# Input stages: four weight sums of a 7-product block scheme become additions, and the fourth is made by two accumulating DMAs

## The reference, cut to what matters

```
h = rms_norm(x, g)                       # 256 x 2048
gate, up = jnp.split(h @ w_in, 2, -1)    # w_in: 2048 x 11264
return (silu(gate) * up) @ w_out
```

## Time and profile before

| | |
|---|---|
| median of 2 runs | 1805.05 us |
| the runs | 1804.71 and 1805.38 us |
| span of the profiled execution | 1802.5 us |
| PE busy | 1797.3 us |
| DVE busy | 1550.1 us |
| ACT busy | 1071.0 us |
| POOL busy | 43.6 us |
| read from HBM | 348.91 MB, 195 GB/s over the span |

### The profile page before, as it was taken

The page is one execution under the profiler, slowest core; times in us unless marked ns, Lnnn a source line. Parts: engine busy times, 40 slices in busy tenths (PEclk is TensorE's granted clock), DMA queues, the critical chain, the costliest instruction groups (busy, mean ns, idle before and its releaser), DMA issues.

```text
span 1802.5 us, 22784 instructions
## 1 busy us (share of the span) xinstructions
PE 1797.3 (100%) x8227; PEld 1491.7 (83%) x8227; DVE 1550.1 (86%) x1614; ACT 1071.0 (59%) x1295; POOL 43.6 (2%) x73
## 2 busy tenths in 40 slices
PE   9999999999999999999999999999999999999999
PEld 8888888888888888888888888888888888888887
DVE  7899999999999887657766666799999999998986
ACT  7566656666665564556556555566666666666553
POOL 0000000000000000111010000000000000000000
PEclk9999999999999999999999999999999999999999
DMA  9565555554446566555545445755566656354654
GB/s 358 214 220 199 207 212 186 196 200 163 140 166 253 189 218 212 198 172 164 164 164 187 143 165 183 257 194 203 191 216 215 215 189 219 104 187 163 240 203 141
DMA packets 178406, 351.95 MB, mean 195 GB/s; under 512 B 7184, under 2 KB 8224, under 8 KB 178080
## 3 DMA queue, kind: packets, MB, share of 16 engines
q1 hardware_dynamic: 178304, 351.02, 55.9%
q10 hardware_dynamic: 32, 0.01, 0.0%
HBM read 348.91 MB, written 2.10 MB: 195 GB/s over the span
## 4 chain that ended last, share of the span: by engine, by line
PE 100%; DVE 0%; ACT 0%; POOL 0%; issue 0%; ACTq 0%; POOLq 0%
PE acc L537 14%; PE acc L539 14%; PE acc L538 13%; PE acc L599 8%; PE acc L598 8%; PE acc L597 8%; PE turn L610 4%; PE turn L611 4%; PE turn L612 4%; PE acc L611 3%; PE acc L612 3%; PE acc L610 3%; PE turn L568 1%; PE turn L714 1%; PE turn L713 1%; PE turn L712 1%
## 5 line engine op out<-in xcount | busy, mean ns | idle before, releaser
L1323 DVE TENSOR_TENSOR w_lo<-w_raw,w_hi 128x1024 fp32r<-128x1024 f32 x167 | 205.0, 1237 | 132.9 <-ACT w_hi L942 132.3
L942 ACT ACTIVATE w_hi<-w_raw 128x1024 fp32r<-128x1024 f32 x166 | 175.4, 1059 | 198.9 <-PE acc L539 177.1
L959 ACT ACTIVATE w_hi<-b 128x1024 fp32r<-128x1024 f32 x200 | 212.6, 1063 | 117.5 <-PE acc L599 75.7
L973 ACT ACTIVATE w_hi<-w_raw 128x1024 fp32r<-128x1024 f32 x176 | 185.3, 1058 | 121.3 <-PE acc L539 88.5
L599 PE MATMUL acc<-w_hi,h_lo 128*128 128x512 f32 x640 | 249.0, 389 | 0.0
L597 PE MATMUL acc<-w_hi,h_hi 128*128 128x512 f32 x640 | 249.0, 389 | 0.0
L598 PE MATMUL acc<-w_lo,h_hi 128*128 128x512 f32 x640 | 249.0, 389 | 0.0
L1344 DVE TENSOR_TENSOR w_lo<-w_raw,w_hi 128x1024 fp32r<-128x1024 f32 x176 | 212.8, 1221 | 32.1 <-ACT w_hi L973 28.5
L1334 DVE TENSOR_TENSOR w_lo<-b,w_hi 128x1024 fp32r<-128x1024 f32 x200 | 236.3, 1218 | 0.0
L959 ACT ACTIVATE w_hi<-w_raw 128x1024 fp32r<-128x1024 f32 x160 | 169.6, 1061 | 91.7 <-PE acc L599 64.1
L1334 DVE TENSOR_TENSOR w_lo<-w_raw,w_hi 128x1024 fp32r<-128x1024 f32 x160 | 193.5, 1220 | 14.7 <-ACT w_hi L959 11.7
(11 more groups left out here) (218 smaller groups left out, 3276.4 us busy)
## 6 DMA issues: line engine op xcount, KB each, us to landing
w_raw<-in_ffn_w_in SPq DMA_DIRECT2D x94, 1024.0 KB, 5.1
w_raw<-in_ffn_w_out SPq DMA_DIRECT2D x88, 1024.0 KB, 5.0
b<-in_ffn_w_in SPq DMA_DIRECT2D x80, 1024.0 KB, 5.1
w_raw<-in_w_in SPq DMA_DIRECT2D x48, 1024.0 KB, 5.0
w_raw<-in_w_out SPq DMA_DIRECT2D x16, 1024.0 KB, 5.0
w_raw<-in_ffn_w_in SPq DMA_DIRECT2D x4, 512.0 KB, 6.6
x_sb<-in_x SPq DMA_DIRECT2D x3, 512.0 KB, 8.7
out_y<-x_sb SPq DMA_DIRECT2D x3, 512.0 KB, 8.5
```

Of the source, the lines that this page charges most:

```text
L942: nc.scalar.activation(w_hi[:, u % RING, 0:count, :], w_raw[:, slot, k0:k0 + count, :], ACT.Copy).then_inc(hi_ready, 1)
L959: nc.scalar.activation(w_hi[:, slot, :, :], in_raw(piece)[:, k0:k0 + UK, :], ACT.Copy).then_inc(hi_ready, 1)
L973: nc.scalar.activation(w_hi[:, u % RING, :, :], src, ACT.Copy).then_inc(hi_ready, 1)
L1323: nc.vector.tensor_tensor(w_lo[:, slot, 0:count, :], w_raw[:, v // 2 % RAW, k0:k0 + count, :], w_hi[:, slot, 0:count, :].bitcast(F32), ALU ...
```

## The change

In the input stages all sums of weights become additions: `t_1 = b_12 + b_11`, `b_12 = b_22 + b_12`, `t_1 = b_22 + t_1`. The signs move to the activation sums (`signed_sums` in place of `activation_sums` for these stages) and to two of the adds of partial products, which become subtractions. The fourth sum, `b_21 + t_1`, is no longer made by DVE. POOL waits until unit 13's `w_lo` is made (the last reader of sum 3) and then issues two DMAs with `accum_op=ADD`, 2 of the 4 rows each, 512 KB, that read B21 from HBM a second time and add it onto `t_1`. ACT waits for each half (`full_sum_landed`) before it converts unit 18 or 19. B21's own load stays, for P2. P4 and P7 change places: P7 is units 16 and 17, P4 units 18 and 19. B12 is now free at 18 and B21 at 11, but the order of the loads becomes ..., B22, B12, B21, U1. DVE splits units 14 to 16 before it adds P6, 17 to 20 before it adds P7, and waits for unit 19's use before it adds the gate bank.

```
-P1, P5, UP0, P2, UP1, P6, P3, P4, P7, UP2 = 4, 6, 8, 9, 11, 12, 14, 16, 18, 20
+P1, P5, UP0, P2, UP1, P6, P3, P7, P4, UP2 = 4, 6, 8, 9, 11, 12, 14, 16, 18, 20
-FREED = {G0: 2, G1: 4, B11: 6, U0: 12, B22: 16, B21: 18, B12: 20, U1: 22}
+FREED = {G0: 2, G1: 4, B11: 6, U0: 12, B22: 16, B12: 18, B21: 11, U1: 22}
...
+                    elif w in (P4, P4 + 1):
+                        act.wait_ge(full_sum_landed[w - P4], at(16, 16 * (IN_LOOPS * n + 1 + later)))
...
-                weight_sum(t_1[:, :, :], b_22[:, :, :], t_1[:, :, :], ALU.subtract)
-                split_in_lo(s_in, i, half, 9, 14)
-                dve.wait_ge(sum_ready, at(4, sums + 3))
-                dve.wait_ge(lo_ready, at(IN_UNITS, u0 + P2 + 2))
-                weight_sum(b_21[:, :, :], b_21[:, :, :], t_1[:, :, :], ALU.subtract)
-                split_in_lo(s_in, i, half, 14, 18)
+                weight_sum(t_1[:, :, :], b_22[:, :, :], t_1[:, :, :], ALU.add)
+                split_in_lo(s_in, i, half, 9, 17)
                 dve.wait_ge(units_used, at(IN_UNITS, u0 + P6 + 2))
                 dve.wait_ge(partial_copied, at(3, copies + 1))
                 add(rows[:, 1, 0, :], partial[0], rows[:, 0, 0, :]).then_inc(partial_copied, 1)
-                split_in_lo(s_in, i, half, 18, 22)
+                split_in_lo(s_in, i, half, 17, 21)
...
-                split_in_lo(s_in, i, half, 22, 23)
+                split_in_lo(s_in, i, half, 21, 23)
+                dve.wait_ge(units_used, at(IN_UNITS, u0 + P4 + 2))
...
+            def full_sums(src, s_in, n):
+                for i in range(IN_LOOPS):
+                    col = (i + 1) * NC
+                    pool.wait_ge(lo_ready, UNIT[s_in] + IN_FIRST + IN_UNITS * i + P6 + 2)
+                    for h in range(2):
+                        k = K_PLAIN + KS + UK * h
+                        nc.gpsimd.dma_start(t_1[:, UK * h:UK * (h + 1), :], src[:, k:k + UK, col:col + NC],
+                                            accum_op=ALU.add).then_inc(full_sum_landed[h], 16)
```

More of the change, by code:

```diff
@@ L62 @@
 IN_RAW = ((G0, 0), (G0, 2), (G1, 0), (G1, 2), (B11, 0), (B11, 2), (T1, 0), (T1, 2), (U0, 0), (B21, 0), (B21, 2),
-          (U0, 2), (T1, 0), (T1, 2), (B22, 0), (B22, 2), (B21, 0), (B21, 2), (B12, 0), (B12, 2), (U1, 0), (U1, 2))
+          (U0, 2), (T1, 0), (T1, 2), (B22, 0), (B22, 2), (B12, 0), (B12, 2), (T1, 0), (T1, 2), (U1, 0), (U1, 2))
 IN_UNITS = len(IN_RAW)
-P1, P5, UP0, P2, UP1, P6, P3, P4, P7, UP2 = 4, 6, 8, 9, 11, 12, 14, 16, 18, 20
-SUM_OF = {P5: 1, P5 + 1: 1, P6: 3, P6 + 1: 3, P4: 4, P4 + 1: 4, P7: 2, P7 + 1: 2}
-FREED = {G0: 2, G1: 4, B11: 6, U0: 12, B22: 16, B21: 18, B12: 20, U1: 22}
+P1, P5, UP0, P2, UP1, P6, P3, P7, P4, UP2 = 4, 6, 8, 9, 11, 12, 14, 16, 18, 20
+SUM_OF = {P5: 1, P5 + 1: 1, P6: 3, P6 + 1: 3, P7: 2, P7 + 1: 2}
+IN_SUMS = 3
+FREED = {G0: 2, G1: 4, B11: 6, U0: 12, B22: 16, B12: 18, B21: 11, U1: 22}
 assert 2 * IN_UNITS % RING == 0 and K_PLAIN == 2 * KT and IN_LOOPS == 2 * IN_PAIRS and KS == KT
@@ L92 @@
 OUT_LANDED = [2 + len(PERIODS)] * 2 + [2 + len(PERIODS) + N_LONG] * 2
-SUMS = 4 * IN_LOOPS + 4 * len(PERIODS)
+SUMS = IN_SUMS * IN_LOOPS + 4 * len(PERIODS)
 ROUNDS = FFN_ITERS
@@ L308, in hybrid_layer_kernel @@
         sum_ready = sem("sum_ready")
+        full_sum_landed = [sem(f"full_sum_landed{h}") for h in range(2)]
         partial_copied = sem("partial_copied")
@@ L456, in ffn @@
                     load(down, a, k, KT, 2, at + X2 + 1)
-                    sp.wait_ge(sum_ready, SUMS * n + 4 * (IN_LOOPS + m + 1))
+                    sp.wait_ge(sum_ready, SUMS * n + IN_SUMS * IN_LOOPS + 4 * (m + 1))
                     load(down, a, j, KT, 0)
@@ L699, in hidden @@
                 form(s_in, u0, half, P3, sum_of(4), banks[1][:, 0, :], False, False)
-                form(s_in, u0, half, P4, block_of(1, 1), banks[0][:, 1, :], False, True)
                 pe.wait_ge(partial_copied, at(3, 3 * IN_LOOPS * n + 2))
                 form(s_in, u0, half, P7, sum_of(3), partial[0], True, True)
+                form(s_in, u0, half, P4, block_of(1, 1), banks[0][:, 1, :], False, True)
                 for v in range(UP2, IN_UNITS):
@@ L951, in split_in_hi @@
                     if w in SUM_OF:
-                        act.wait_ge(sum_ready, at(4, SUMS * n + SUM_OF[w]))
+                        act.wait_ge(sum_ready, at(IN_SUMS, SUMS * n + SUM_OF[w] + IN_SUMS * later))
+                    elif w in (P4, P4 + 1):
+                        act.wait_ge(full_sum_landed[w - P4], at(16, 16 * (IN_LOOPS * n + 1 + later)))
                     elif piece < B11:
@@ L967, in split_out_hi @@
                     if made:
-                        act.wait_ge(sum_ready, SUMS * n + 4 * IN_LOOPS + made)
+                        act.wait_ge(sum_ready, SUMS * n + IN_SUMS * IN_LOOPS + made)
                     else:
@@ L1034, in copy_m1 @@
                 else:
-                    act.wait_ge(sum_ready, SUMS * n + 4 * (IN_LOOPS + m + 1))
+                    act.wait_ge(sum_ready, SUMS * n + IN_SUMS * IN_LOOPS + 4 * (m + 1))
                 act.wait_ge(units_used, UNIT[s_out] + period_at(m) + Q1 + 1)
@@ L1426, in hidden @@
                 dve.wait_ge(block_landed[B12 - B11], landed)
-                weight_sum(t_1[:, :, :], b_12[:, :, :], b_11[:, :, :], ALU.subtract)
+                weight_sum(t_1[:, :, :], b_12[:, :, :], b_11[:, :, :], ALU.add)
                 split_in_lo(s_in, i, half, 4, 5)
                 dve.wait_ge(block_landed[B22 - B11], landed)
-                dve.wait_ge(sum_ready, at(4, sums + 1))
-                weight_sum(b_12[:, :, :], b_22[:, :, :], b_12[:, :, :], ALU.subtract)
+                dve.wait_ge(sum_ready, at(IN_SUMS, sums + 1))
+                weight_sum(b_12[:, :, :], b_22[:, :, :], b_12[:, :, :], ALU.add)
                 split_in_lo(s_in, i, half, 5, 9)
                 dve.wait_ge(lo_ready, at(IN_UNITS, u0 + P5 + 2))
-                weight_sum(t_1[:, :, :], b_22[:, :, :], t_1[:, :, :], ALU.subtract)
-                split_in_lo(s_in, i, half, 9, 14)
-                dve.wait_ge(sum_ready, at(4, sums + 3))
-                dve.wait_ge(lo_ready, at(IN_UNITS, u0 + P2 + 2))
-                weight_sum(b_21[:, :, :], b_21[:, :, :], t_1[:, :, :], ALU.subtract)
-                split_in_lo(s_in, i, half, 14, 18)
+                weight_sum(t_1[:, :, :], b_22[:, :, :], t_1[:, :, :], ALU.add)
+                split_in_lo(s_in, i, half, 9, 17)
                 dve.wait_ge(units_used, at(IN_UNITS, u0 + P6 + 2))
@@ L1446, in hidden @@
                 add(rows[:, 0, 1, :], partial[0], rows[:, 1, 0, :]).then_inc(partial_copied, 1)
-                add(rows[:, 1, 0, :], partial[1], rows[:, 1, 0, :])
+                nc.vector.tensor_tensor(rows[:, 1, 0, :], partial[1], rows[:, 1, 0, :], ALU.subtract)
                 dve.wait_ge(partial_copied, at(3, copies + 3))
-                add(rows[:, 1, 1, :], partial[1], rows[:, 0, 1, :]).then_inc(partial_added, 1)
+                nc.vector.tensor_tensor(rows[:, 1, 1, :], partial[1], rows[:, 0, 1, :],
+                                        ALU.subtract).then_inc(partial_added, 1)
                 if ending:
                     round_act(n, 0)
-                split_in_lo(s_in, i, half, 22, 23)
+                split_in_lo(s_in, i, half, 21, 23)
+                dve.wait_ge(units_used, at(IN_UNITS, u0 + P4 + 2))
                 dve.wait_ge(partial_added, at(1, done))
@@ L1472, in activation_wide, with signed_sums @@
                 return [wide[:, KS * half:KS * (half + 1), t * P:(t + 1) * P] for half in range(2) for t in range(TT)]
+            def signed_sums(raw, a_11, a_21, a_12, a_22):
+                link(nc.vector.tensor_tensor(raw[:, 0], a_21, a_22, ALU.subtract))
+                nc.vector.tensor_tensor(raw[:, 2], a_11, a_21, ALU.subtract)
+                link(nc.vector.tensor_tensor(raw[:, 1], raw[:, 0], a_11, ALU.subtract))
+                nc.vector.tensor_tensor(raw[:, 3], a_12, raw[:, 1], ALU.add).then_inc(s_raw_ready, 1)
             def activation_sums(raw, a_11, a_21, a_12, a_22):
@@ L1527, in ffn @@
                     split_lo(s_in, 8, 10, PARTS_D)
-                    activation_sums(s_raw, *blocks)
+                    signed_sums(s_raw, *blocks)
                     split_lo(s_in, 10, 11, PARTS_D)
@@ L1570, in begin_products @@
                 u0, at = period_at(m), UNIT[s_out] + period_at(m)
-                made = SUMS * n + 4 * (IN_LOOPS + m)
+                made = SUMS * n + IN_SUMS * IN_LOOPS + 4 * m
                 b_11, b_12, b_22 = w_raw[:, 0, 0:UK, :], w_raw[:, 1, 0:UK, :], w_raw[:, 1, UK:KT, :]
@@ L1903, in _ @@
             pool.wait_ge(col_ready, 3)
+            full_sums(tiled(ffn1_w_in), IN1, 0)
             pool.wait_ge(units_used, UNIT[QKV])
@@ L1929, in _ @@
                 nc.gpsimd.tensor_tensor(x2, temps[2], temps[3], ALU.add).then_inc(qk_normed, 1)
+            full_sums(tiled(ffn2_w_in), IN2, 1)
 _INS = ["x", "ffn1_norm", "ffn1_w_in", "ffn1_w_out", "mix_norm", "w_in", "a_q_norm", "a_k_norm", "b_q_norm",
```

## The result

The changed kernel takes 1984.52 us (1984.45 to 1984.59, 2 runs) against 1805.05 us: a ratio of 1.0995, 95% interval 1.0976 to 1.1014. It is slower by 179.5 us, 9.0 us for each of the 20 periods. The profiled execution has a span of 1982.7 us, 180.2 us more than before.

A forecast was written before the change was run, and what follows sets the result against it. PE, busy 1797.3 of 1802.5 us, was taken to bound the kernel. Half 1 landing late stalls PE 2.4 us in each of 20 periods, 48 us: span 1850.5, plus 2.6 around it, 1853 us; range 1803 to 1930.

The forecast's parts named there:

- PE bounds the kernel, DVE's relief is worth 0: Input stages: PE never waits for a weight, so removing 20 DVE sums of 2283 ns, 45.7 us, gains 0.
- The new order: P7 before P4: DVE's add of P6 ends 0.7 us before PE asks for it at unit 16; cost 0.
- The cover: Time from POOL's wait ending to when half 0 and half 1 must have landed: 7.3 and 8.7 us.
- POOL's issue, 1.04 us, and half 0's transfer, 4.9 us: POOL issues half 0 at 329.1; counted as 1 MB of reads, it lands at 334.0, in time by 1.4 us.
- Half 0 goes out at 329.1, half 1 at 330.2: POOL issues the two halves one behind the other, 1.04 us for each, range 0.37 to 2 us.
- rival 2: Halves go one at a time, or adder at half rate (1957 us); stall over 4 us, 1885 to 2000 us; chance 0.28.
- the case without it: The forecast's own case: stall of 1 to 4 us a period, 1825 to 1885 us; chance 0.43.
- Contention, 2.6 us: B22's load shares the DMA engines with half 1, moving its landing from 336.6 to 339.2, late by 2.4 us.
- Rival 3, the clock: PE's clock falls in the stalls, perhaps 1 to 3 us a period on top; no chance of its own, within 0.28.

## Why the prediction was wrong

The forecast was 1853 us with a range to 1930; 1984.5 us came. Step by step:

- *PE bounds the kernel, DVE's relief is worth 0*: right. The run with plain copies takes away the same DVE work and ends at 0.9995 of before.
- *The new order costs 0*, with 0.7 us left at unit 16: right. In the changed kernel the add of P6 ends at 289.92 and unit 16's first weight load starts at 290.66; and the run with the fourth sum on DVE takes as long as before.
- *The cover*, 7.3 and 8.7 us: right. Half 0 landed 6.4 us after the split and did not stall PE. With half 1 at 9.1 us the stalls were small; at 16.1 us PE stood for 7.46 us, close to 16.1 - 8.7.
- *POOL's issue, 1.04 us, and half 0's transfer, 4.9 us*: 5.9 us from the split by the sum; measured, half 0 landed 6.0 us after the issue's start and 6.4 us after the split, which POOL followed after 0.35 us. The sum takes a half for 1 MB of reads, which no row of the kernel before shows. In time it came out right: accumulating halves move about 205 GB/s where a load moves about 400, and the size of the packets is not the reason, since the loads' packets (351.02 MB in 178304) are as small as the accumulating ones (20.97 MB in 10880). That it is a second read is the reading that fits a factor of two; no view shows the reads.
- *"Half 0 goes out at 329.1, half 1 at 330.2"*: this step failed. Half 1 went out 6.36 us after half 0, not 1.04, since with a store of 1024 POOL issued an accumulating half only when the one before had landed. A store of 2048 brings the issues to 0.73 us apart and removes 153 us. I had one half at a time in rival 2, but with 0.28 beside slow adders, when the kernel text gave the parameter. With 0.43 for the case without it, I took the unknown at its kind end.
- *Contention, 2.6 us*: its kind was right and the size depends on the moment. Half 1 met three loads in place of one: 9.4 us to land against 5.9 with the loads held. In the case for which I had computed it (both halves at once) it was smaller than I said: landing at 9.1 us after the split, not 11.1, and PE's waits of 18.4 us in all, not 48. There half 1 took 8.1 us from its issue, against 7.7 with the loads held (289.63 to 297.37), so the term was 0.4 us in these periods and not 2.6. The forecast for that case, 1853 us, compares with 1831.
- *Rival 2's price*: with the prediction's own terms half 1 goes out at 334.0 + 1.04 and lands 4.9 us later at 339.9, with contention at 342.5, a stall of 5.8 us: 20 x 5.8 = 116 us, 1921 us. The waits were 131 us. In the period shown half 1 landed 16.1 us after the split where these terms give 14.4: the issue came 0.8 us later than their sum says (6.7 us after the split, not 5.9), and contention was 3.4 us in place of 2.6.
- *Rival 3, the clock, "perhaps 1 to 3 us a period"*: 2.2 us, 44 us in all. I named it and said that it was left in the range, but no row stood behind these 1 to 3 us, and no term of it went into the upper end. Rivals 2 and 3 are not independent: the long wait is what brings the low clock (0.51 behind 7.46 us of standing, 1.000 over the span when PE was kept busy through it). Added, 1921 + 44 = 1965, they come near the result.

What the runs say of the store can be put as an estimate from the packets of POOL's queue: 272 for an accumulating half (10880 in 40), 144 for an accumulating quarter (11520 in 80) or a plain half (5760 in 40). A limit on the packets under way anywhere from 432 to 543 gives all four outcomes at 1024: two accumulating halves (544) do not go out together, three quarters (432) do, four (576) don't, two plain halves (288) do. Twice such a limit takes the two accumulating halves of the run with 2048. That the store's size is the cause is shown (1984.52 to 1831.08 us by this parameter alone); that it works by this count is not. The fourth quarter does not fit it: with quarter 0 landed at 285.2, 288 packets would be under way and 144 more would fit, but it went out at 288.19, behind the landing of quarter 1.

## What to carry to other kernels

Before a second DMA of POOL is counted as running right behind the first, make sure that it is issued before the first has landed; here, with `dynamic_dma_scratch_size=1024`, two plain halves went out back to back (1.45 us for both) and two accumulating ones 6.36 us apart. When an engine has no waits, taking work from its neighbours is worth nothing (with the plain copies DVE had the same relief, at 0.9995 of the time before), and a new transfer in the chain is priced by latency against its window, at the moment when other loads run. A wait of several microseconds on TensorE is priced with the slow matmuls behind it: here 2.2 us on 7.5.

## What the runs showed of the hardware that I had not expected

- With `dynamic_dma_scratch_size=1024` POOL had one accumulating DMA of 512 KB under way (the second 6.36 us behind the first), or three of 256 KB (three issues in 2.67 us), or at least two plain ones of 512 KB (two in 1.45 us). With 2048 it had two accumulating ones of 512 KB (two in 2.46 us). The fourth of 256 KB went out only when the second had landed, 2.1 to 3.6 us after the first.
- Accumulating transfers from HBM onto SBUF moved about 205 GB/s with the DMA engines over 90% busy, where plain ones moved about 400.
- Transfers that came late to busy engines paid much: an accumulating one of 256 KB took 8.4 us beside three loads of 1 MB, and one of 512 KB 9.4 against 5.9 alone.
- After PE stood for 7.5 us, ten matmuls ran about 0.43 us apart (granted clock 0.51); after 4.0 us of standing, seven came 0.23 us apart (clock 1.00) and only then eight at 0.43 (0.53); PE kept busy through the wait had none (clock 1.000 over the span).
- POOL's issues did not slow DVE: with the plain copies DVE was busy for 383.5 of the 416.5 us of the earlier trace rows beside them, and its split of a unit stayed at 1.22 us.
